# Key and value pages: two neighbouring tokens to a partition, one page on each half of the partitions

## The reference, cut to what matters

```python
kp = cache_k[i, page_table].reshape(db, past_len, MOBA_HEADS, HEAD_DIM)
vp = cache_v[i, page_table].reshape(db, past_len, MOBA_HEADS, HEAD_DIM)
...
k_mean = jnp.mean(kb.astype(jnp.float32), axis=3)          # kb: blocks of 256 tokens
gate = jnp.einsum('bhtd,bhnd->bhtn', qh, k_mean)
_, sel = lax.top_k(gate, 3)
logits = q . k * scale - slope[h] * (q_pos - s_pos)         # s_pos: the token's position
out = softmax(logits over the chosen blocks and the own one) @ v
```

## Time and profile before

| what | us |
|---|---|
| median of 3 runs | 1142.82 (1141.63 to 1145.15) |
| the profiled execution's own time | 1140.18 |
| its span | 1138.3 |
| PE busy in the span | 1080.7 (95%) |
| DVE busy | 704.4 (62%) |
| ACT busy | 537.8 (47%) |
| POOL busy | 295.4 (26%) |
| DMA queue of SP | 118402 packets, 174.61 MB, 46.2% of 16 engines |

### The profile page before, as it was taken

One profiled execution on the slowest core, in us unless ns is written; L12 is line 12 of the kernel. 1 busy time (PEld: TensorE's weight loads), 2 busy tenths in 40 slices (PEclk: granted clock), 3 DMA queues, 4 the chain that ended last, 5 costly groups with the idle time before them and its releaser, 6 DMA issues.

```text
span 1138.3 us, 20143 instructions
## 1 busy us (share of the span) xinstructions
PE 1080.7 (95%) x7047; PEld 974.3 (86%) x7047; DVE 704.4 (62%) x1187; ACT 537.8 (47%) x856; POOL 295.4 (26%) x283
## 2 busy tenths in 40 slices
PE   7999999878999998999999999989999999999996
PEld 6999899556666666588999999979998899999996
DVE  4763565677777777568666653375565866665344
ACT  3337612366666665535444433352333644443324
POOL 8400135105667777133000001042003400000111
PEclk8989989899999999999999999999999999999999
DMA  7444200478989996534444434325435344444321
GB/s 207 147 148 153 76 1 1 157 220 305 317 306 308 303 306 202 178 126 143 150 149 147 147 132 149 130 75 173 154 127 152 123 150 151 152 154 141 130 82 46
DMA packets 120882, 182.60 MB, mean 160 GB/s; under 512 B 6224, under 2 KB 61615, under 8 KB 120750
## 3 DMA queue, kind: packets, MB, share of 16 engines
q1 hardware_dynamic: 118402, 174.61, 46.2%
q0 software_dynamic: 2416, 7.16, 2.1%
HBM read 176.12 MB, written 5.63 MB: 160 GB/s over the span
## 4 chain that ended last, share of the span: by engine, by line
PE 81%; DVE 11%; ACT 3%; issue 3%; DMA 1%; SPq 0%; DVEq 0%; ACTq 0%
PE bank L1766 75%; PE bank L2130 4%; DVE kTl L1179 2%; DVE lo L1172 1%; DMA xtok<-x_sample 1%; ACT hi L765 1%; DVE xres L1617 1%; DVE sbias L1491 1%; DVE gs L1487 1%; DVE sbias L1482 1%; DVE xl L1624 1%; DVE xres L1179 0%; PE bank L2356 0%; PE bank L2261 0%; PE bank L2161 0%
## 5 line engine op out<-in xcount | busy, mean ns | idle before, releaser
L1766 PE MATMUL bank<-xh,hi 128*128 128x320 f32 x1184 | 370.5, 313 | 9.8 <-DVE xl L1624 5.1
L1766 PE MATMUL bank<-xl,hi 128*128 128x320 f32 x1184 | 367.4, 310 | 0.0
L1766 PE MATMUL bank<-xh,lo 128*128 128x320 f32 x1184 | 367.4, 310 | 0.0
L1172 DVE TENSOR_TENSOR lo<-raw,hi 128x2048 fp32r<-128x2048 f32 x102 | 240.9, 2362 | 187.5 <-ACT hi L765 187.5
L765 ACT ACTIVATE hi<-raw 128x2048 fp32r (+2 forms) x124 | 217.9, 1758 | 117.5 <-PE bank L1766 115.9
L1766 PEld LDWEIGHTS bank<-xh,hi 128*128 128x128 f32 x1184 | 223.8, 189 | 15.1 <-issue 7.2
L1766 PEld LDWEIGHTS bank<-xl,hi 128*128 128x128 f32 x1184 | 224.0, 189 | 0.1
L1766 PEld LDWEIGHTS bank<-xh,lo 128*128 128x128 f32 x1184 | 223.7, 189 | 0.0
L1766 PE MATMUL bank<-hh,hi 128*128 128x320 f32 x416 | 129.1, 310 | 1.3 <-DVE hraw L1179 1.3
L1766 PE MATMUL bank<-hh,lo 128*128 128x320 f32 x416 | 128.4, 309 | 0.0
L1766 PE MATMUL bank<-hl,hi 128*128 128x320 f32 x416 | 128.4, 309 | 0.0
(11 more groups left out here) (407 smaller groups left out, 1529.3 us busy)
## 6 DMA issues: line engine op xcount, KB each, us to landing
raw<-w_up SPq DMA_DIRECT2D x44, 1024.0 KB
kring<-cache_k SPq DMA_DIRECT2D x88, 256.0 KB, 3.8
vring<-cache_v SPq DMA_DIRECT2D x84, 256.0 KB, 4.9
raw<-w_down SPq DMA_DIRECT2D x8, 2048.0 KB
raw<-w_in_mix SPq DMA_DIRECT2D x6, 2048.0 KB
raw<-cache_v SPq DMA_DIRECT2D x44, 256.0 KB, 4.6
raw<-cache_k SPq DMA_DIRECT2D x40, 256.0 KB, 3.7
raw<-w_in_sc SPq DMA_DIRECT2D x8, 1024.0 KB
```

Of the source, the lines that this page charges most:

```text
L1172: dve.tensor_tensor(lo[:, p], weight(n)[:, :, 256 * p:256 * p + 256], hi[:, p], ALU.subtract)\
L1766: return pe.matmul(out, lhsT, rhs, start=start, stop=stop, **kw)
```

## The change

Before, a page's DMA writes all 128 partitions: token p of the page goes to partition p, 2 KB each, and the two pages of a pair lie beside each other in the free dimension. Now the first page of a pair goes to partitions 0 to 63 and the second to partitions 64 to 127; a partition gets the two neighbouring tokens 2r and 2r + 1, which are 4 KB in a row in the cache and 4 KB in a row in the buffer. A DMA still moves 256 KB. `keyb` is made in the same order: column 128j + 64u + r of a block is the position of token 2r + j of its page u. Everything else is as before, as many instructions of each kind and shape.

```diff
             def load_pair(out, cache, landed, n):
                 for u in range(2):
                     x = listed[2 * n + u]
-                    sp_.dma_start(out[:, u, :], cache[bass.ds(x, 1)].rearrange("o p h d -> (o p) (h d)")).then_inc(s[landed], 16)
+                    sp_.dma_start(out[64 * u:64 * u + 64], cache[bass.ds(x, 1)].rearrange("o (r j) h d -> (o r) j (h d)", j=2))\
+                        .then_inc(s[landed], 16)
...
                     for i in range(4):
-                        dve.tensor_scalar(keyb[:, PAGE * i:PAGE * i + PAGE], c128[:, :], spread[:, i:i + 1], spread[:, 4:5],
-                                          ALU.subtract, ALU.mult)
+                        pair = keyb[:, 2 * PAGE * (i // 2):2 * PAGE * (i // 2) + 2 * PAGE].rearrange("p (j u r) -> p u j r", j=2, u=2)
+                        dve.tensor_scalar(pair[:, i % 2], c128[:, :].rearrange("p (r j) -> p j r", j=2), spread[:, i:i + 1],
+                                          spread[:, 4:5], ALU.subtract, ALU.mult)
```

## The result

| | median us | runs | ratio to before |
|---|---|---|---|
| before | 1142.8 | 1141.63 to 1145.15 (4) | |
| after | 1178.0 | 1166.32 to 1178.56 (4) | 1.0309 [1.0271, 1.0347] |

The change costs 3.1%, some 35 us. The profiled execution after took 1178.56 us, its span 1176.7 us, 38.4 more than before. First, the page of the kernel after: as many instructions as before, the same bytes, 16,384 packets fewer, and pages that land late.

A forecast was written before the change was run, and what follows sets the result against it. PE set the pace, with DMA 10% from full. Pages at 232 GB/s would come 44.2 us late; added to the profiled 1140.18 us that made 1184.4, plus 2.6 to the median 1187.0 us, range 1140 to 1226.

The forecast's parts named there:

- The bound moves to DMA, the stages behind move along: Page stage: loads get less than the 303 GB/s needed; later stages stay unchanged and begin 44 us later.
- R = 232 GB/s: Page stage: rate of pages sent to one half, taken from the 64-partition store `y_s`; bounds 205 to 334 GB/s.
- With 1.5 us for the last landing: End of the page loads: 1.5 us added to the transfer time, putting the last values at 513.9 us, 44.2 late.
- Keys and values are used when they land, with no lead left: End of page stage: lateness counted from today's uses at 440.7 and 469.7 us, giving 41.7 and 44.2 us.
- PE waits for pages at the transposes: Page stage, expected sign: PE waits for key or value landings at the transposes, ACT at the value splits; no size given.
- Nothing from `keyb`: Four DVE instructions of 340 ns at 227 us: taken as 0, at most +1.4 us, once.
- Issue time of 0.11 us more: SP's page issues: each may take 0.11 us more, 15.7 instead of 12.2 us a round; nothing added.
- rival 3: Page stage: PE's granted clock falls too, +23 us on top of the 44 for 1210 us; above 1222 us, chance 0.07.
- rival 4: Page loads: 4 KB runs and fewer packets speed the transfer, at most a fraction of 9.3 us; 1139 us, chance 0.07.
- rival 5: Page loads: a partition's two tokens still go as two 2 KB packets; same forecast time, no chance of its own.
- rivals 1 and 2: Page loads: engines out of step, 334 GB/s, 1143 us, chance 0.16; or half in step, 274 GB/s, 1149 us, within 0.70.

The follow-up runs named there:

- even_odd: The changed kernel, but the first page of a pair goes to the even partitions and the second to the odd; 1141.2 us, ratio 1.0003 to before.
- lluu: The changed kernel with each group's four pages issued in the order lower, lower, upper, upper half; 1190.4 us, ratio 1.0450 to the kernel before.

## Why the prediction was right, point by point

- *The bound moves to DMA, the stages behind move along.* Right: 668.60 and 668.57 us behind the last split. The forecast was +44 us; the span rose by 38.4, the medians by 35.
- *R = 232 GB/s, from a store at a full share.* A little low: 246, at a share of 1.04. By itself, at 246, the working gives the last values at 250.3 + 247.2 + 1.5 - 469.7 = +29 us, 15 less than the forecast.
- *"With 1.5 us for the last landing", and a split as soon as that is in.* This step was off the other way, by 9 us. The last unit that was split the moment it landed was not the last one, 63 counting from 0, but 51, the second behind the last keys (by the landing signals in the trace file): landed at 478.79, split at 478.82 (before: landed at 432.48, split at 441.86). From 248.99 us on, the 208 pages up to it (54.5 MB) take to 470.6 at 246 GB/s; its last signal came 8.2 us later, not 1.5, and 5.9 us after the first of its 32 signals (2.0 before). And from its split to the last split 29.3 us passed, 27.9 before, where the 24 pages left would take 25.6 at 246: in this tail the loads no longer set the pace, and the DMA share fell to 0.90, 0.73, 0.58 and 0.20 from 490 us on. These two gaps, 6.7 and 3.7 us, less the 1.3 by which the stage began earlier, are the 9.
- *Keys and values are used when they land, with no lead left.* Nearly right: the last keys landed at 474.54 and were used at 477.58, 3.0 us later, where it had been 10.9 (429.75 and 440.68). R too low and the landing too short had opposite signs, and the total came out closer than either term: that part is luck.
- *PE waits for pages at the transposes.* It did so for 0.5 us of the whole kernel. The waits are ACT's, as the forecast also had it, and reach PE through `kTl`.
- *Nothing from `keyb`.* Right: 340 ns each, as in the earlier trace rows.

```profile
L1407 DVE TENSOR_SCALAR keyb<-c,spread x4: 336/340/343, 225.6 to 226.4; 128x128 f32<-128x128 f32 x4
```

- *Issue time of 0.11 us more.* It was 0.14 to 0.16 more, and hidden, as `even_odd` shows.
- *The clock* (rival 3). Right to leave it out of the sum: the granted clock was 0.87 to 0.96 in the windows of the stage where it had been 1.00. From the first key issue above to the last split PE was busy for 19.0 us more than before (220.0 against 200.9) and idle for 20.7 more. The DMA share stays at 1.04 in the windows from 290 to 450 us, so PE's slower stretches filled time in which it would have waited.
- *Longer rows pay* (rival 4), *two packets of 2 KB all the same* (rival 5) and *in step or not* (rivals 1 and 2): `even_odd` has the longer rows on both halves and gains nothing. The 16,384 packets fewer are one packet instead of two for every partition of the 256 pages, so rival 5 is out. The rate neither rose through the stage nor reached 283.
- *The Trainium skill*, "SBUF — State Buffer", section "Door 1: The DMA port swizzle (why `[64,N]` ≈ `[32,N]`)", told the direction and nearly the size: its 218 GB/s for partitions 0 to 63 are close to what `lluu` shows (220 to 224 from 290 to 450 us). Its section "Can I just issue two DMAs to hit both halves?" allows some 6% over one half; on its 218 that would be 231, an estimate from the two sections' figures. Alternating pages got 246, and up to 343 with other copies among them (17 of it the copies), so the runs here don't bear out that two halves always serialize.

## What to carry to other kernels

Before a layout is changed for longer rows, ask whether anything waits for a load, and how near the DMA engines are to full: here no engine waited for a load at full pace and the margin was 10%, so there was little to win and 3% to lose. Let each DMA cover both halves of the partitions; if a partition must hold neighbouring rows, give the two pages the even and the odd partitions, which cost nothing here. And a wide load queued beside narrow ones isn't safe: half of the pages narrow was at least as slow as all.

## What the runs showed that I had not expected

- Half of the pages wide again: 1186 and 1187 us, no better than the change; the rate fell from 259 to 220 GB/s in one execution.
- Another order moved the rate of the same transfers from 246 to 221 GB/s.
- Adding 25 copies of 128 KB to a queue that was full made it faster: 1.0182 and 1.0234 of the time before against 1.0309, with windows up to 343 GB/s.
- At an unchanged mean rate the landing signals of a key group drifted apart, from 5.1 to 8.0 us, and the last signal of unit 51 came 8.2 us later than its bytes at that rate.
